# Fewer page DMAs ahead of a norm's sum, and a reordered start: squares off GpSimd, a later norm, first weights in halves, 28 products of ones

## The reference

```python
def rms_norm(x, g):
    xf = x.astype(jnp.float32)
    y = xf * lax.rsqrt(jnp.mean(xf * xf, axis=-1, keepdims=True) + EPS)
    return (y * g.astype(jnp.float32)).astype(x.dtype)

def swiglu_ffn(x, g, w_in, w_out):
    h = rms_norm(x, g) @ w_in
    a, b = jnp.split(h, 2, axis=-1)
    return (jax.nn.silu(a) * b) @ w_out
...
xp = xp + 0.5 * swiglu_ffn(xp, norm_ffn_a[i], w_ffn_a_in[i], w_ffn_a_out[i])
...
qp, kp, vp, qip, kip, wip = attn_project(xp, norm_mix[i], *ap)      # begins with rms_norm
# the samples' indexer reads its cached keys through the page table
ki_past = cache_kidx[page_table].reshape(B, PAST_LEN, IDX_DIM)
```

## Time and profile before

| | us |
|---|---|
| median of 3 runs | 2470.29 (2469.33 to 2484.86) |
| the profiled execution, its own time | 2470.15 |
| its span, first to last instruction | 2468.4 |
| TensorE busy in the span | 2351.3 (95%) |
| VectorE busy | 1766.4 (72%) |
| ScalarE busy | 1100.1 (45%) |
| GpSimd busy | 465.5 (19%) |

### The profile page before, as it was taken

One profiled execution on the slowest core, in us unless ns is written; L12 is line 12 of the kernel. 1 busy time (PEld: TensorE's weight loads), 2 busy tenths in 40 slices (PEclk: granted clock), 3 DMA queues, 4 the chain that ended last, 5 costly groups with the idle time before them and its releaser, 6 DMA issues.

```text
span 2468.4 us, 46321 instructions
## 1 busy us (share of the span) xinstructions
PE 2351.3 (95%) x18654; PEld 2213.7 (90%) x18654; DVE 1766.4 (72%) x2604; ACT 1100.1 (45%) x1951; POOL 465.5 (19%) x365
## 2 busy tenths in 40 slices
PE   6999997998789999999999999999998979999999
PEld 6999997887456999999999999999896779999999
DVE  7975974674464589478888478777767974795794
ACT  5543542244433355245455245323565542453452
POOL 3000058323500600000400000400474304000000
PEclk9999998997689999999999999999998989999999
DMA  3322233224523222322322222233362012222223
GB/s 123 103 94 94 103 102 108 91 94 120 187 88 137 69 74 94 106 86 99 106 86 95 95 91 96 98 136 119 116 234 103 1 52 103 86 98 93 100 91 100
DMA packets 52876, 251.45 MB, mean 102 GB/s; under 512 B 8352, under 2 KB 16672, under 8 KB 32864
## 3 DMA queue, kind: packets, MB, share of 16 engines
q1 hardware_dynamic: 46432, 219.73, 25.6%
q0 software_dynamic: 6272, 29.37, 3.6%
HBM read 233.58 MB, written 15.49 MB: 101 GB/s over the span
## 4 chain that ended last, share of the span: by engine, by line
PE 84%; DVE 7%; POOL 3%; ACT 3%; issue 2%; DMA 0%; DVEq 0%; ACTq 0%; POOLq 0%
PE acc L640 31%; PE acc L520 22%; PE acc L490 8%; PE acc L1385 4%; PE acc L2792 3%; POOL kic L741 2%; PE acc L626 2%; PE acc L2861 1%; PE acc L1758 1%; ACT wh L385 1%; PE acc L1479 1%; DVE wl L426 1%; PE acc L1794 1%; PE acc L1782 1%; PE acc L2910 1%
## 5 line engine op out<-in xcount | busy, mean ns | idle before, releaser
L640 PE MATMUL acc<-xa,wh 128*128 128x268 f32 (+1 forms) x2240 | 436.1, 286 | 1.9 <-ACT sq L949 1.7
L640 PE MATMUL acc<-xe,wh 128*128 128x268 f32 (+1 forms) x2240 | 436.4, 286 | 0.5 <-DVE wl L1076 0.2
L385 ACT ACTIVATE wh<-raw 128x2048 fp32r<-128x2048 f32 x114 | 218.2, 1914 | 408.0 <-PE acc L520 303.0
L640 PEld LDWEIGHTS acc<-xa,wh 128*128 128x128 f32 x2240 | 348.9, 188 | 4.0 <-ACT sq L949 2.1
L640 PEld LDWEIGHTS acc<-xe,wh 128*128 128x128 f32 x2240 | 348.3, 188 | 1.4 <-DVE scr L1108 0.7
L640 PE MATMUL acc<-xa,wl 128*128 128x268 f32 (+1 forms) x1120 | 319.8, 286 | 0.0
L640 PE MATMUL acc<-xe,wl 128*128 128x268 f32 (+1 forms) x1120 | 319.8, 286 | 0.0
L426 DVE TENSOR_TENSOR wl<-raw,wh 128x2048 fp32r<-128x2048 f32 x104 | 251.2, 2416 | 67.0 <-ACT wh L385 66.6
L520 PE MATMUL acc<-gh,wh 128*128 128x268 f32 (+1 forms) x1408 | 288.7, 286 | 10.4 <-DVE wl L426 8.9
L520 PE MATMUL acc<-gl,wh 128*128 128x268 f32 (+1 forms) x1408 | 287.3, 285 | 0.0
L520 PE MATMUL acc<-gh,wl 128*128 128x268 f32 (+1 forms) x1408 | 287.1, 285 | 0.0
(11 more groups left out here) (554 smaller groups left out, 4947.2 us busy)
## 6 DMA issues: line engine op xcount, KB each, us to landing
raw<-in_w_ffn_in SPq DMA_DIRECT2D x88, 1024.0 KB, 4.9
raw<-in_w_ffn_out SPq DMA_DIRECT2D x32, 768.0 KB, 4.2
raw<-in_w_ssd_in SPq DMA_DIRECT2D x21, 1024.0 KB, 4.8
raw<-in_w_ffn_out SPq DMA_DIRECT2D x32, 640.0 KB, 3.8
raw<-in_w_attn_in SPq DMA_DIRECT2D x9, 1024.0 KB, 5.0
kic<-in_kpages SPq DMA_DIRECT2D x64, 128.0 KB
xT<-in_state_ssm SPq DMA_DIRECT2D x8, 1024.0 KB, 7.0
out_hs<-xT SPq DMA_DIRECT2D x8, 1024.0 KB, 3.9
```

Of the source, the lines that this page charges most:

```text
L385: nc.scalar.activation(wh[:, slot], raw[:, slot], ACT.Copy).then_inc(wh_ready, 1)
L640: mm = nc.tensor.matmul(bank(n, number), w[:, slot, c:c + P], x_pair(f, low, i)[:, m0:m0 + hc], start=(number in (1, 2, 5) and i == 0 and ...
```

## The change

- `pool_sumsq`, in `out01`: six page DMAs ahead of the first square and three ahead of each other one, 27 instead of 40; `pool_attention` issues the remaining 37 (24 before).
- GpSimd makes no squares for the first norm. ScalarE makes all eight (`act_first_squares`), VectorE adds them up (`dve_first_sums`).
- The first norm's product stands in the second plain chunk, at its fourth input tile (`FIRST_SUM_AT`), and uses the PSUM slot of the first chunk. For this ScalarE copies the first chunk's result out of PSUM (`act_first_out`); the gate and the gated product of that chunk are made from the copy (`first_gate`, `first_hidden`).
- The first weights are split in two halves of four input tiles each (`act_first_weights`, `dve_first_weights`), and the order on ScalarE and VectorE at the start is written anew.
- TensorE multiplies the ones with themselves 28 times (`WARM`) ahead of the first chunk, into a bank that nobody reads then.

```diff
+FIRST_SUM_AT = 3
+WARM = 28
...
             if section == "out01":
-                pool_index_pages(pool, 5 * n, 5 * n + 5)
+                pool_index_pages(pool, 3 * n + 3 if n else 0, 3 * n + 6)
...
-        return (first + 1) % 2, first
+        return (first + 1 if k else 0) % 2, first
...
-        pe.wait_ge(epilogue_done, first + CREDIT)
+        pe.wait_ge(epilogue_done, first + CREDIT + (0 if k else 1))
...
-            pe.wait_ge(wl_ready, n + 1)
+            if n:
+                pe.wait_ge(wl_ready, n + 1)
+            else:
+                pe.wait_ge(x_mixed, 1)
             for at, kt in enumerate(PAIRED):
-                if j == 0 and at == NORM_AT:
+                if (j, at) == ((0, NORM_AT) if f else (1, FIRST_SUM_AT)):
                     pe_norm(pe, k)
+                if n == 0 and at == 4:
+                    pe.wait_ge(wl_ready, 1)
...
+        if f == 0 and g == 0:
+            for _ in range(WARM):
+                nc.tensor.matmul(acc[:, 7, 0:P], ones[:], ones[:], start=True, stop=True)
...
+    def first_half(w, half):
+        return w[:, 0].rearrange("p (a k c) -> p a k c", a=2, k=4)[:, :, 2 * half:2 * half + 2]
+    def act_first_weights(act, half):
+        act.wait_ge(w_loaded[0], 16)
+        nc.scalar.activation(first_half(wh, half), first_half(raw, half), ACT.Copy).then_inc(wh_ready if half else x_made, 1)
...
+    def act_first_out(act):
+        act.wait_ge(chunk_done, 1 + CREDIT)
+        nc.scalar.copy(halves(silu_a[:, 0]), pair(0, 0)).then_inc(x_made, 1)
+        nc.scalar.copy(halves(hid[:, 0]), pair(0, 1)).then_inc(epilogue_done, 1)
...
+    def dve_first_sums(dve, chain):
+        dve.wait_ge(x_made, 9 + DT)
+        chain.link(nc.vector.tensor_tensor(squares[:, 0:4], squares[:, 0:4], squares[:, 4:8], ALU.add))
+        chain.link(nc.vector.tensor_tensor(squares[:, 0:2], squares[:, 0:2], squares[:, 2:4], ALU.add))
+        nc.vector.tensor_tensor(ssum[:], squares[:, 0], squares[:, 1], ALU.add).then_inc(ssum_ready, 1)
...
-        pool_index_pages(pool, 5 * DT, S // 2 * NPG)
+        pool_index_pages(pool, 3 * DT + 3, S // 2 * NPG)
...
-        act_round(act, 0, 0, 0)
+        act.wait_ge(const_ready, 2)
+        nc.scalar.activation(rstd[:, 0:1], epsc[:], ACT.Copy)
+        act_first_weights(act, 0)
         act.wait_ge(gains_loaded, 16)
...
-        pool_first_squares(pool, chain)
```

More of the change, by code:

```diff
@@ L688, in act_first_pair, with act_first_squares, dve_first_weights, dve_first_low @@
             nc.scalar.activation(xgain[:, i, half * N:(half + 1) * N], xT[:, t], ACT.Copy, scale=gains[:, 0, t:t + 1]).then_inc(x_made, 1)
[L689 removed]
+        act.wait_ge(x_made, 2 * i + 3)
         nc.scalar.activation(x_pair(0, 0, i)[:, 0:2 * N], xgain[:, i], ACT.Copy).then_inc(xh_ready, 1)
[L692 to L694 removed]
+    def act_first_squares(act):
+        for t in range(DT):
             nc.scalar.activation(squares[:, t], xT[:, t], ACT.Square).then_inc(x_made, 1)
     def act_first_mixed(act, i):
[L699 removed]
+        act.wait_ge(x_mixed, i + 2)
         nc.scalar.activation(x_pair(0, 0, i)[:, 2 * N:4 * N], xmix[:, i], ACT.Copy).then_inc(xh_ready, 1)
[L702 removed]
+    def act_first_out(act):
+        act.wait_ge(chunk_done, 1 + CREDIT)
+        nc.scalar.copy(halves(silu_a[:, 0]), pair(0, 0)).then_inc(x_made, 1)
+        nc.scalar.copy(halves(hid[:, 0]), pair(0, 1)).then_inc(epilogue_done, 1)
+    def dve_first_weights(dve, half):
+        dve.wait_ge(wh_ready if half else x_made, 1)
+        nc.vector.tensor_tensor(first_half(wl, half), first_half(raw, half), first_half(wh, half).bitcast(F32),
+                                ALU.subtract).then_inc(wl_ready if half else x_mixed, 1)
+    def dve_first_low(dve, i):
         dve.wait_ge(xh_ready, i + 1)
@@ L706, in dve_first_pair, with dve_first_mix @@
                                 ).then_inc(xl_ready, 1)
+    def dve_first_mix(dve, chain, i):
         b = [xgain[:, i, s * H:(s + 1) * H] for s in range(4)]
@@ L970, in act_blocked @@
             act_std(act, k)
-            if f == 0:
-                for i in range(1, 4):
-                    act_first_mixed(act, i)
             if f == 1:
                 act_pair_high(act, f, 3, 1)
-            silu(base)
+            if f:
+                silu(base)
             high_a11(n0)
@@ L979, in act_blocked @@
             high_s31(n0)
+            if f == 0:
+                silu(base)
             high_hidden(base)
@@ L1147, in dve_blocked @@
         if g == 0:
-            if f != 1:
-                dve_rstd(dve, chain, k)
[L1150 to L1160, removed]
+            if f == 0:
+                sums_13(n0)
+                sum_2(n0)
+                low_a11(n0)
+                low_s2(n0)
+                dve_rstd(dve, chain, k)
+                first_gate()
+                low_s31(n0)
+                sum_4(n0)
+                first_hidden()
+            else:
+                if f != 1:
+                    dve_rstd(dve, chain, k)
+                plain_gate(0)
+                sums_13(n0)
+                sum_2(n0)
+                plain_hidden(0)
+                low_a11(n0)
+                low_s2(n0)
+                low_s31(n0)
+                sum_4(n0)
             low_hidden(base)
@@ L3545, in _ @@
     def _(act):
-        act_round(act, 0, 0, 0)
+        act.wait_ge(const_ready, 2)
+        nc.scalar.activation(rstd[:, 0:1], epsc[:], ACT.Copy)
+        act_first_weights(act, 0)
         act.wait_ge(gains_loaded, 16)
-        for i in range(3):
+        act_first_pair(act, 0)
+        act_first_weights(act, 1)
+        for i in range(1, 4):
             act_first_pair(act, i)
[L3550 to L3553, removed]
         act_round(act, 1, 0, 0)
-        act_first_mixed(act, 0)
+        act_first_squares(act)
+        for i in range(4):
+            act_first_mixed(act, i)
+        act_first_out(act)
         for what in order:
@@ L3582, in _ @@
         nc.vector.memset(epsc[:], EPS).then_inc(const_ready, 1)
-        dve_rest(dve, 0, 0, 0)
+        dve_first_weights(dve, 0)
+        dve_first_low(dve, 0)
+        dve_first_weights(dve, 1)
+        dve_first_mix(dve, chain, 0)
+        dve_first_low(dve, 1)
+        dve_first_mix(dve, chain, 1)
+        dve_first_low(dve, 2)
+        dve_first_low(dve, 3)
+        dve_first_mix(dve, chain, 2)
+        dve_rest(dve, 1, 0, 0)
+        dve_first_mix(dve, chain, 3)
+        dve_first_sums(dve, chain)
         for i in range(4):
-            dve_first_pair(dve, chain, i)
-        dve_rest(dve, 1, 0, 0)
-        dve_first_mixed(dve, 0)
+            dve_first_mixed(dve, i)
         for what in order:
```

23 lines of the change are left out of this document (9 added, 14 removed).

## The result

The changed kernel took 2447.37 us in the median of four runs (2439.61 to 2448.57), the kernel before 2469.81 in the median of four beside them: the ratio is 0.9888, with a 95% interval of 0.9845 to 0.9931, so 1.1% faster. That is the ratio of the means, 2445.73 and 2473.34; the ratio of the two medians is 0.9909. The forecast time was 2447.4, but it was given as "within 1%". The profiled execution took 2446.40 (span 2444.6), 23.75 less than the profiled one of before; the sum had said 22.75.

A forecast was written before the change was run, and what follows sets the result against it. It took TensorE's stand of 17.2 us at the second norm, then the start, as what could be reached. Gains of 19.5 and 3.25 make 22.75, so 2470.15 becomes 2447.4 us; own range 2445.6 to 2450, wider range 2442.5 to 2454.

The forecast's parts named there:

- Part 1: At the second norm: 13 fewer page DMAs ahead of GpSimd's sum, TensorE's wait gone, 19.5 us gained.
- Part 2: At the start: squares leave GpSimd, saving VectorE 9.07 us of contention; VectorE's own sums cost 4.4.
- Sum of the start: Start up to the blocked products: TensorE goes on at 46.4 instead of 51.19; 3.25 us gained after 1.5 clock loss.
- Part 4: First norm moved to the second chunk: TensorE waits 0.8, off the path; a new VectorE wait of 0.75.
- Part 5: First chunk: the 28 products of ones may keep the clock full, but are costed at nothing in either direction.
- (b): Rival at the second norm: GpSimd falls one tile behind, TensorE stands 3 to 4, 2451 to 2454 us; chance 0.14.
- (c): Rival at the cached dots: the 37 put-off page DMAs become the new wait, up to 2485 us; chance 0.03.
- (a): Rival at the entry: clock stays up and sums of squares are cheaper, 2445.5 us or a little less; chance 0.27.
- How the numbers follow: Closing step on whole time: chances 0.27 faster by over 1%, 0.70 within 1%, 0.03 slower by over 1%.

The follow-up runs named there:

- e7: The changed kernel with all 64 page DMAs issued behind the second norm's sum, none ahead of its squares; 2467.99 us, ratio 1.0010 to the kernel before.
- e10: The kernel before with only the page DMAs changed (6 ahead of the first square, 3 ahead of each other, 37 behind the sum), run again for a profile; 2463.68 us.

## Why the prediction was right, and where it was wrong

**Right, by its steps.** Part 1: the sum ends at 396.30, which is 399.90 on the old scale (forecast 399.9), and the add was held by L428 as said. The point of 422.16 stands at 398.97; without the start's 3.60 that is 19.6 (forecast 19.5). The 23 issues between 336 and 396 us took 1.66 each with all gaps, and six of them 2.09 to 3.05 beside L428: held, as the rows of before had it, and not free, as the Trainium skill (SBUF — State Buffer, "Who interferes with whom") infers. All of them are indirect and read their row numbers from a tile (`irow`); whether an issue without such a read is held, no run here shows. The 37 behind took 52.5 (forecast 53), and the cover was 8.0, not 9, since a landing takes 1.6. Part 2: 8.96 (9.07) for the contention, 4.38 (4.4) for the sums. Sum of the start: TensorE goes on at 46.45 (46.4); the first pair came at 9.40, not 9.7, as the weights were there at 5.76 instead of 6.22. The clock fell at the entry and cost 1.5, as in the sum; 0.4 of it came back in the next steps, which the sum did not have, so the start gave 3.60 (3.25). Part 4 and Part 5 as said: a wait of 0.42 at the first norm, and ones that bring nothing.

**Rivals.** (b) and (c) have their switch points now: four issues for a tile instead of three cost 11.0, by the mechanism of (b) but at more than its price; 64 issues behind the sum cost a wait of 25 at the dots, by that of (c). At three and 37 neither was met, the first by 0.3 us only. (a) named a clock that does not fall at the entry. Of the eight profiles with this order at the entry e7's is the one behind whose second wait the clock stayed up; there TensorE came to the norm's product 1.1 earlier than in the changed kernel (395.52 against 396.59). The larger differences of the clock lie in the attention part, which (a) did not name.

**The step that failed** is "How the numbers follow", with the line on which it rests. It took a measurement to tell about 1% from no change, laid the line at 2445.6, 1.8 us below the forecast, and gave 0.70 to "within 1%", with an own range of 4.4 us, as though a run were known to that. The runs showed two other things. First, 0.9% is well told from no change: the three comparisons of the changed kernel have intervals of 0.2 to 0.4% to either side, and none of them reaches 1. Second, runs of one kernel lie much further apart than 1.8 us: fifteen runs of the changed kernel lie between 2438.3 and 2461.7, 73 of the kernel before between 2462.6 and 2484.9. So the side of the line was left to which runs fell into the comparison. The 1.1% is the ratio of means of four runs each, and one run of 2484.86 of the kernel before is in it; without that run the means give 0.9904, and the medians give 0.9909 with it. That the median of 2447.37 meets the forecast time of 2447.4 is luck to that digit, since the four runs lie 9 us apart.

The sum itself was 1.0 short: 0.35 in the start, 0.1 in Part 1, 0.1 up to the cached dots and 0.5 behind them (23.3 up to there, 23.8 at the end), which no term had. That alone does not cross the line, 23.75 of 2470.15 being 0.96%. The granted clock of the attention part, worth some 4 us between two profiles of the same kernel, stood in neither the sum nor the range. All runs together have medians of 2446.3 and 2468.2, 21.9 or 0.9% apart, while the three comparisons gave 1.1, 1.05 and 0.8%: whether the change is a little over or under 1% is not settled by these runs.

## What to carry to other kernels

Count the DMA issues that an engine makes between two of its sums against the spacing of what the sums wait for, held issues included: three for a tile fitted here by 0.3 us, the fourth cost 11; what is put off must be issued before its reader comes (8 us of cover here). Where TensorE waits at a handover, order the short copy that frees its PSUM ahead of the conversions that only later steps need. And before giving a chance to one side of a line, look at how far runs of the same kernel lie apart and at the granted clock of each: a forecast nearer to the line than that says little about the side. Look, too, at what a ratio is made of: in a mean of four one long run counts for almost 4 us.

## What was not expected of the hardware

The clock takes two courses over the same instructions with the same waits: after the 0.74 at 511 us, four products took 0.76 or 1.19, and in the latter case TensorE stayed at half clock for 34 us, though busy in 33.06 of them; after the 0.87 at 685 us, 1.28 or 1.92 for sixteen. The Trainium skill, TensorE: Matmul & The Clock Gate, "HAM oscillation — how this bites in real kernels", tells of a clock that falls in waits for loads; the row of e10 shows it low where there were hardly any waits.

GpSimd's adds and VectorE's residuals of weights hold each other: the add that took 1.31 alone took 3.28 beside L428, and L428, 2.29 undisturbed, took 2.96 beside the add.
